# A decoder layer's opening: modulation sums on TensorE column tiles, and the first four FFN units taken row chunk by row chunk

## The reference

```python
cond = silu(c)
mod = cond @ w_ada + b_ada                    # 1024 x 9216: nine shifts, scales and gates
sh1, sc1, gt1, sh2, sc2, gt2, sh3, sc3, gt3 = split(mod, 9)
u = rms_norm(x, g_ffn1) * (1 + sc1) + sh1
a, b = split(u @ w_ffn1_in, 2)                # 1024 x 5632
h = x + 0.5 * gt1 * ((silu(a) * b) @ w_ffn1_out)
```

## Time and profile before

| | |
|---|---|
| three runs | 1361.37, 1361.68 and 1363.66 us, median 1361.68 us |
| the profiled execution | 1360.55 us |
| its span, first to last instruction | 1358.5 us |
| TensorE busy | 1261.8 us, 93% |
| VectorE busy | 668.1 us, 49% |
| ScalarE busy | 658.8 us, 48% |
| chain that ended last | TensorE 85%, VectorE 6%, ScalarE 5%, SyncE's queue 2%, DMA 1% |

### The profile page before, as it was taken

One profiled execution on the slowest core, in us unless ns is written; L12 is line 12 of the kernel. 1 busy time (PEld: TensorE's weight loads), 2 busy tenths in 40 slices (PEclk: granted clock), 3 DMA queues, 4 the chain that ended last, 5 costly groups with the idle time before them and its releaser, 6 DMA issues.

```text
span 1358.5 us, 17931 instructions
## 1 busy us (share of the span) xinstructions
PE 1261.8 (93%) x6505; PEld 1015.8 (75%) x6505; DVE 668.1 (49%) x953; ACT 658.8 (48%) x1152; POOL 69.7 (5%) x101
## 2 busy tenths in 40 slices
PE   2699999999997999999888978899799999999998
PEld 1588888887775777777667857677578888888887
DVE  6766666665443563665374345465453333333221
ACT  5566666665553696555684332653432232222221
POOL 3000000000110000000302121001100000000000
PEclk8699999999999999999998988999999999999999
DMA  9467776776552222222221120163223333343321
GB/s 322 114 186 186 184 187 184 187 199 178 147 156 62 62 78 78 63 62 78 78 70 47 48 70 25 61 182 117 83 62 99 102 93 93 98 124 97 114 79 31
DMA packets 279955, 152.36 MB, mean 112 GB/s; under 512 B 7877, under 2 KB 275294, under 8 KB 279902
## 3 DMA queue, kind: packets, MB, share of 16 engines
q1 hardware_dynamic: 275678, 149.54, 39.6%
q10 hardware_dynamic: 4224, 2.10, 0.5%
HBM read 145.31 MB, written 6.29 MB: 112 GB/s over the span
## 4 chain that ended last, share of the span: by engine, by line
PE 85%; DVE 6%; ACT 5%; SPq 2%; issue 2%; DMA 1%; ACTq 0%; DVEq 0%
PE region L1278 12%; PE region L1279 12%; PE region L1280 12%; PE tail L1278 12%; PE tail L1279 12%; PE tail L1280 12%; PE region L1434 2%; SPq L366 1%; PE region L1296 1%; PE region L1582 1%; PE region L1572 1%; PE region L1586 1%; PE region L1420 1%; PE region L1469 1%; PE region L1307 1%
## 5 line engine op out<-in xcount | busy, mean ns | idle before, releaser
L505 ACT ACTIVATE w_hi<-raw 128x1024 fp32r<-128x1024 f32 (+1 forms) x181 | 201.6, 1115 | 493.2 <-PE region L1280 242.4
L857 DVE TENSOR_TENSOR w_lo<-raw,w_hi 128x1024 fp32r<-128x1024 f32 (+1 forms) x181 | 234.9, 1298 | 270.7 <-ACT w_hi L505 269.1
L1278 PE MATMUL region<-u_hi,w_hi 128*128 128x512 f32 x672 | 265.7, 395 | 3.7 <-DVE w_lo L857 3.7
L1280 PE MATMUL region<-u_hi,w_lo 128*128 128x512 f32 x672 | 261.6, 389 | 0.0
L1279 PE MATMUL region<-u_lo,w_hi 128*128 128x512 f32 x672 | 261.6, 389 | 0.0
L1278 PE MATMUL tail<-u_hi,w_hi 128*128 128x512 f32 x344 | 145.7, 423 | 8.2 <-DVE w_lo L857 8.2
L1278 PEld LDWEIGHTS region<-u_hi,w_hi 128*128 128x128 f32 x672 | 126.1, 188 | 32.8 <-issue 4.7
L1279 PEld LDWEIGHTS region<-u_lo,w_hi 128*128 128x128 f32 x672 | 126.1, 188 | 28.3 <-issue 2.4
L1280 PEld LDWEIGHTS region<-u_hi,w_lo 128*128 128x128 f32 x672 | 126.1, 188 | 26.4
L1278 PE MATMUL tail<-g_hi,w_hi 128*128 128x512 f32 x352 | 141.1, 401 | 0.0
L1280 PE MATMUL tail<-g_hi,w_lo 128*128 128x512 f32 x352 | 139.0, 395 | 0.0
(11 more groups left out here) (285 smaller groups left out, 1531.4 us busy)
## 6 DMA issues: line engine op xcount, KB each, us to landing
raw<-in_w_ffn_in SPq DMA_DIRECT2D x176, 256.0 KB, 3.4
ada_raw<-in_w_ada SPq DMA_DIRECT2D x56, 512.0 KB, 5.1
raw<-in_w_in SPq DMA_DIRECT2D x90, 256.0 KB, 3.3
raw<-in_w_ffn_out SPq DMA_DIRECT2D x32, 384.0 KB, 4.6
raw<-in_w_ffn_out SPq DMA_DIRECT2D x32, 320.0 KB, 3.6
ada_early<-in_w_ada SPq DMA_DIRECT2D x8, 1024.0 KB, 12.0
kept_gates<-rstd SPq DMA_DIRECT2D x16, 256.0 KB, 3.6
gates<-kept_gates SPq DMA_DIRECT2D x16, 256.0 KB, 4.2
```

The source lines that it names most:

```text
L505: act.activation(w_hi[:, slot % 2, 0:k, :], raw[:, slot, 0:k, :], ACT.Copy).then_inc(hi_ready, 1)
L857: dve.tensor_tensor(w_lo[:, slot % 2, 0:k, :], raw[:, slot, 0:k, :], w_hi[:, slot % 2, 0:k, :].bitcast(f32), ALU.subtract).then_inc(lo_rea ...
L1278: pe.matmul(bank(b), wh, xh, start=start and n == 0, stop=False)
L1280: ins = pe.matmul(bank(b), wl, xh, start=False, stop=stop and n == k - 1)
```

## The change

Nothing outside the opening and the start of FFN1's first product is changed, apart from semaphore counts.

**Loads.** x comes first, with one semaphore for each block of 128 tokens. The small vectors follow. The eight early pieces come in the order scale, shift, scale, shift (256 columns each). Behind every second piece come two row chunks of the first four units, in four loads of 128 KB: 128 rows of four 128-column blocks.

**Root mean square.** ScalarE squares x as it lies in memory, with the sum along the row; Ln and Exp give the rough root for 512 tokens in a 128 x 4 tile, VectorE refines it, and four matmuls spread it. VectorE now copies the transposed x to `hT`.

**Early sums.** TensorE multiplies cond, broadcast to 32 columns, with a row chunk of a piece, in one of four column tiles of 32 columns; eight matmuls per piece, two in each tile. ScalarE copies the 128 x 256 result, and two matmuls with a column of 1/32 put the sums on partitions. `ada_sum` and the scaling and halving of early pieces are gone.

**Four units.** Units 0 to 3 are worked through with the row chunk outermost: `first_half(k, 0)` is chunk k of units 0 and 1, `first_half(k, 1)` of units 2 and 3, six matmuls each. The chunks of a pair have their weights and activations split in pairs on ScalarE and VectorE. The five places that the split weights of a chunk go through lie in the two `w` slots.

**Behind them.** The units of the pairs j = 0 and 1 are then finished together. With j = 0 ScalarE and VectorE split units 4 and 5; with j = 1 they split none; from j = 2 on they split two each as before (unit 6 first).

```diff
--- before.py
+++ after.py
+FIRST = 4
+F1_IN = KD - FIRST
...
+def first_tile(k):
+    return FIRST * ((k + 2) % 5)
+def early_col(a):
+    return PIECE * (a // 2) + (0 if a % 2 else D)
...
@@ sync @@
-            sp.dma_start(ada_early[:, 0], w_ada_v[:, :, 0:PIECE]).then_inc(ada_early_in[0], 16)
             for b in range(NB):
-                sp.dma_start(x_nat[:, b, :], x[0, b * P:(b + 1) * P, :]).then_inc(x_in, 16)
-            for q in range(1, EARLY):
-                sp.dma_start(ada_early[:, q], w_ada_v[:, :, q * PIECE:(q + 1) * PIECE]).then_inc(ada_early_in[q], 16)
+                sp.dma_start(x_nat[:, b, :], x[0, b * P:(b + 1) * P, :]).then_inc(x_in[b], 16)
...
-            for u in range(RAW):
-                load(F1_IN, 0, u)
+            for a in range(EARLY):
+                sp.dma_start(ada_early[:, a], w_ada_v[:, :, early_col(a):early_col(a) + PIECE]).then_inc(ada_early_in[a], 16)
+                if a % 2:
+                    for k in (a - 1, a):
+                        for half in range(2):
+                            sp.dma_start(raw_tiles[:, FIRST * k + 2 * half:FIRST * k + 2 * half + 2, :],
+                                         ffn_in_v[0][:, k, half * FF:half * FF + 2 * P].rearrange("p (t n) -> p t n", n=P))\
+                                .then_inc(first_in[k // 2], 16)
...
             for i in laps(sp, KF // 2):
+                if is_static(i) and i == 0:
+                    load(F1_IN, 0, 3 + RAW)
+                    for u, used in ((0, 2), (1, 5)):
+                        sp.wait_ge(lo_ready, used)
+                        load(F1_IN, 0, u + RAW)
+                        load_late(u, u)
+                    sp.wait_ge(lo_ready, KD)
+                    load(F1_IN, 0, 2 + RAW)
                 for u in range(4):
...
@@ scalar: ffn @@
-                        split_hi(phase, i, 2 * jj + 2)
-                        act.wait_ge(unit_done, phase + 2 * j + 1)
+                        lead = 2 * jj + 2 if f or not is_static(j) or j > 1 else 4 if j == 0 else None
+                        if lead is not None:
+                            split_hi(phase, i, lead)
+                        if lead == 2 * jj + 2:
+                            act.wait_ge(unit_done, phase + 2 * j + 1)
+                        elif j == 0:
+                            act.wait_ge(unit_done, KD)
+                        else:
+                            act.wait_ge(first_done, 1)
...
-                        split_hi(phase, i, 2 * jj + 3)
+                        if lead is not None:
+                            split_hi(phase, i, lead + 1)
@@ scalar: opening @@
+            act.preload_act_table_set("natural_log_exp_and_others")
+            for b in range(NB):
+                act.wait_ge(x_in[b], 16)
...
+                act.activation(x_sq[:, :], x_nat[:, b, :], ACT.Square, accum_out=tok["sum"][:, b:b + 1]).then_inc(tok_root, 1)
...
+            def early_part(a):
+                act.wait_ge(early_ps, a + 1)
+                if a >= 2:
+                    act.wait_ge(early_cols, a - 1)
+                act.activation(parts[:, a % 2, :], bank(6 + a % 2)[:, 0:PIECE], ACT.Copy).then_inc(early_copied, 1)
+            def first_hi(k):
+                act.wait_ge(first_in[k // 2], 64)
+                if k >= 5:
+                    act.wait_ge(unit_done, k - 4)
+                act.activation(wh_tiles[:, first_tile(k):first_tile(k) + FIRST, :],
+                               raw_tiles[:, FIRST * k:FIRST * k + FIRST, :], ACT.Copy).then_inc(hi_ready, 1)
+            early_part(0)
+            early_part(1)
+            for k in range(0, KD, 2):
+                first_hi(k)
+                first_hi(k + 1)
+                act.wait_ge(early_mod, k + 2)
+                for k1 in (k, k + 1):
+                    act.wait_ge(normed_ready, k1 + 1)
+                    act.activation(u_hi[:, k1, :], work[:, k1 % 2, :], ACT.Identity,
+                                   bias=mod[:, SH[0] * KD + k1:SH[0] * KD + k1 + 1]).then_inc(u_hi_ready, 1)
+                if k + 2 < KD:
+                    early_part(k + 2)
+                    early_part(k + 3)
@@ vector: opening @@
...
+            for k in range(0, KD, 2):
+                first_scale(k)
+                scaled(0, k)
+                early_columns(k + 1)
+                scaled(0, k + 1)
+                first_lo(k)
+                low(0, k)
+                first_lo(k + 1)
+                low(0, k + 1)
+                dve.wait_ge(u_lo_ready, k + 2)
@@ tensor: opening @@
...
+            def early_piece(a):
+                pe.wait_ge(ada_early_in[a], 16)
+                if a >= 2:
+                    pe.wait_ge(early_copied, a - 1)
+                for k in range(KD):
+                    t = k % 4
+                    ins = pe.matmul(bank(6 + a % 2)[32 * t:32 * t + 32, 0:PIECE],
+                                    cond[:, k:k + 1].to_broadcast([P, 32]), ada_early[:, a, k, :],
+                                    start=k < 4, stop=k >= 4, tile_position=(0, 32 * t))
+                ins.then_inc(early_ps, 1)
+            def early_totals(a):
+                pe.wait_ge(early_copied, a + 1)
...
+                for n in range(2):
+                    col = early_col(a) // P + n
+                    ins = pe.matmul(bank(5 - a % 2)[:, col:col + 1], parts[:, a % 2, n * P:(n + 1) * P], share[:, 0:1],
+                                    start=True, stop=True)
+                ins.then_inc(early_cols, 1)
+            def first_half(k, j):
+                if j == 0:
+                    pe.wait_ge(lo_ready, k + 1)
+                    pe.wait_ge(u_lo_ready, k + 1)
+                xh, xl = u_hi[:, k, :], u_lo[:, k, :]
+                for ab in range(2):
+                    tile = first_tile(k) + 2 * ab + j
+                    wh, wl, dst = wh_tiles[:, tile, :], wl_tiles[:, tile, :], bank(2 * j + ab)
+                    pe.matmul(dst, wh, xh, start=k == 0, stop=False)
+                    pe.matmul(dst, wh, xl, start=False, stop=False)
+                    ins = pe.matmul(dst, wl, xh, start=False, stop=k == KD - 1)
+                return ins
+            early_piece(0)
+            early_piece(1)
+            early_totals(0)
+            early_totals(1)
             for k in range(KD):
+                more = k % 2 == 0 and k + 2 < KD
+                ins = first_half(k, 0)
...
+                if more:
+                    early_piece(k + 2)
+                    early_piece(k + 3)
+                ins = first_half(k, 1)
+                ins.then_inc(first_done if k == KD - 1 else unit_done, 1)
+                if more:
+                    early_totals(k + 2)
+                    early_totals(k + 3)
             ffn_in(0, F1_IN)
```

More of the change, by code:

```diff
@@ L159, in build @@
         eps = sb("eps", [P, 1])
+        share = sb("share", [P, 1])
         ssq = sb("ssq", [P, S])
@@ L170, in build @@
             ada_early = sb("ada_early", [P, EARLY, KD, PIECE], stack=s)
+            parts = sb("parts", [P, 2, PIECE], stack=s)
+            x_sq = sb("x_sq", [P, D], stack=s)
+            tok = {n: sb("tok_" + n, [P, NB], stack=s) for n in ("sum", "mean", "rstd", "tmp")}
         with ExitStack() as s:
@@ L222, in bank @@
             return t[:, k * S:(k + 1) * S]
+        raw_tiles = raw.rearrange("p s k n -> p (s k) n")
+        wh_tiles, wl_tiles = (t.rearrange("p s k n -> p (s k) n") for t in (w_hi, w_lo))
         def heads(ap):
@@ L555, in ffn @@
                                 ada_scale(ada_raw[:, k], ada_scaled, (ada_in[k], 16 * (j + 1)))
-            act.wait_ge(masks, 9)
+            act.wait_ge(masks, 10)
             act.wait_ge(c_ps, 1)
[L560 to L565, removed]
@@ L576, in _ @@
             ffn(0, F1_IN)
-            for i in laps(act, KD // 2, 0, 1):
+            for i in laps(act, KD // 2):
                 for oo in range(2):
@@ L858, in split_lo @@
                                   w_hi[:, slot % 2, 0:k, :].bitcast(f32), ALU.subtract).then_inc(lo_ready, 1)
[L860 to L865, removed]
-                        dve.wait_ge(done, KD * q + k)
-                        ins = dve.scalar_tensor_tensor(acc, piece[:, k, :], cond[:, k:k + 1], acc, ALU.mult, ALU.add)
-                    ins.then_inc(done, 1)
             def halve(acc, piece, done, q):
@@ L1008, in _ @@
-            split_lo(F1_IN, 0, 0)
-            split_lo(F1_IN, 0, 1)
-            dve.wait_ge(early_ps, 1)
-            dve.wait_ge(vec_ready, 2)
-            dve.tensor_tensor(mod[:, 0:LATE], bank(5)[:, 0:LATE], vec[:, 0:LATE], ALU.add).then_inc(early_mod, 1)
-            dve.wait_ge(early_mod, 1)
-            norm(0)
+            for t in range(2 * NB):
+                b, half = t // 2, t % 2
+                dve.wait_ge(x_ps, t + 1)
+                dve.tensor_copy(hT[:, 4 * half:4 * half + 4, b * P:(b + 1) * P], heads(bank(t % 4))).then_inc(h_ready, 1)
@@ L1370, in _ @@
-            ins.then_inc(early_ps, 1)
```

(19 more changed lines are left out.)

201 lines of the change are left out of this document (111 added, 90 removed).

## The result

The changed kernel takes 1349.1 us (median; the runs lie between 1347.7 and 1351.4) against 1361.5 us before: ratio 0.9909, 95% interval 0.9889 to 0.9929. The forecast was 1348. The profiled execution took 1349.81 us, its span 1348.1.

A forecast was written before the change was run, and what follows sets the result against it. TensorE was taken to bound the kernel except in the opening, held by loads and VectorE. Ten units done at 98.3 instead of 111.7 us save 13.4: 1360.55 becomes 1347.1, as a median 1348; 80% range 1338 to 1363.

The forecast's parts named there:

- First FFN matmul: Opening, TensorE: the first FFN matmul starts at 22.5 us, 30 us earlier than before.
- Column tiles: Early sums on TensorE: four column tiles overlap fully, a piece taking 0.86 us at clock 1.00, 1.7 at half clock.
- the rival: Early sums: column tiles don't overlap fourfold; one after another a piece takes 3.4 us at 1.00, time 1366; chance 0.12.
- The loop: Opening, from pair to pair of chunks: TensorE's queue plus 3.9 us of VectorE's chain, 8.8 us a pair.
- The distance that the loads would have given: Opening: 7.6 us between pairs, a sign that the loads and not the loop bound it.
- Four units: End of the opening on TensorE: units 0 to 3 done at 57.2 us; 54 all at 1.00, up to 66.
- The new wait: Behind unit 5: unit 6 waits for late pieces, TensorE idle from T + 11.4 to T + 17.6 except a 0.86 us sum.
- T: The time at which the first four units are done on TensorE, forecast at 57.2 us.
- ten units: Units 0 to 9 done on TensorE: forecast T + 41.1 = 98.3 us, against 111.68 before.
- The half clock: Behind the pause after unit 5: TensorE's clock falls, and unit 6 and 7 lose 1.6 us.
- moves with it: Behind ten units: the same work, bound by TensorE, was to shift by the same 13.4 us.
- sum 2: The second late sum on TensorE, by which ten units are done; forecast 98.3 us, 111.68 before.

The follow-up runs named there:

- e3_lo_first: Changed kernel with VectorE making both `w_lo` of a pair of chunks ahead of the columns; 1348.87 us, ratio 0.9912 to before.
- e5_filled: Changed kernel with five unused f32 matmuls put into TensorE's pause ahead of the first late sum; 1345.56 us, ratio 0.9866 to before.
- a_again: The changed kernel run again without any edit; 1347.56 us, ratio 0.99 to before.
- e1_late_ahead: Changed kernel with scaling of late pieces 0 and 1 ahead of the first silu, their halving also earlier; 1341.97 us, ratio 0.9863 to before.
- e6_both: Changed kernel with the edits of e1_late_ahead and e3_lo_first together; 1344.86 us, ratio 0.9885 to before.
- e4_x_late: Changed kernel with SyncE asking for early pieces 0 and 1 ahead of x; 1351.3 us, ratio 0.9902 to before.
- e2_one_tile: Changed kernel without column tiles, a piece's eight matmuls one after another over 128 columns; 1367.08 us, ratio 1.0026 to before.

## Why the prediction was right, point by point

- **First FFN matmul.** Predicted 22.5 us, found 21.81, 21.55, 21.77 and 21.66 in four executions of this opening. The last link was as told: piece 1 seen late, its sums, then VectorE's columns, `work`, `w_lo` and `u_lo` (2.85 us for 2.9). The links ahead of it were off both ways: piece 1 was seen at 16.78 for 15.9, but its matmuls took 1.0 us for 1.7 and the sums 1.2 for 2.0, since TensorE's clock was 1.00 there (windows 16.7 to 19 us) and not 0.50.
- **Column tiles.** Predicted 0.86 us a piece for full overlap; found 1.93/2 = 0.97 at clock 1.00, against 7.07/2 = 3.5 without. The price of the rival was right too: 1366 predicted, 1367.08 found with the overlap gone. The Trainium skill, "TensorE: Matmul & The Clock Gate" (Part 3, Measured speedup vs the span model), has 2.38-fold for three column tiles; four gave 3.66-fold here, which lies between that share and full overlap. Of the 2 us that its share would have added, about 0.9 came (0.97 for 0.86 us, eight pieces).
- **The loop.** Predicted 8.8 us a pair, found 8.8. That the sum came out so well is luck. From the first sum to chunk 4's first matmul the forecast set 3.9 us for VectorE's chain; it took 3.3 (37.53 to 40.81), and the terms ahead of it were 0.6 us longer than forecast:

```profile
37.53 0.16 DVE L1087 TENSOR_TENSOR mod<-region,vec 128x2 f32<-128x2 f32 x1 [4.39 <-PE region L1495]
```

And the forecast had it that the chain counts and chunk k + 1 does not. In fact TensorE is at work on chunk k + 1 until 0.22 us before the chain ends, so the loop is TensorE's queue almost alone, with 0.15 us of VectorE's chain (e3_lo_first). The distance that the loads would have given, 7.6, does not appear.
- **Four units.** Predicted 57.2, found 55.2: 0.7 us from the first matmul, and 1.4 us of half clock in the first loop (10.2 against 8.8) in place of 2.9. The first six matmuls ran at 0.50 as forecast (windows 21.8 to 24.6 us), the pieces behind them mostly did not in this execution (0.94 from 24.6 to 27.8).
- **The new wait.** Predicted from T: piece 3 asked for at T + 8.1, unit 6 at T + 17.6, ten units at T + 41.1. With T = 55.2 that is 63.3, 72.8 and 96.3; found 63.29, 73.2 and 96.43. Of all steps this one was nearest: most of its links had a row of the same form in the trace before, and what had to be found was only who stands behind whom on ScalarE. One link was another: unit 6 was to wait for VectorE's split, which ended at 72.2, and it waited for the sum ahead of it, which at 0.50 took 2.08 us in place of 0.86 and ended at 73.2. The half clock cost 2.0 to 2.4 us (e5_filled) where 1.6 were set.
- **What the prediction left out.** It said that all behind ten units "moves with it". It does not quite. Between sum 2 and the end of the span, 1.5 to 5.3 us of the lead over the profiled execution of before are lost in all eight kernels:

| | lead at sum 2 | lead at the end | given back |
|---|---|---|---|
| the changed kernel | 15.25 | 10.4 | 4.8 |
| a_again | 14.0 | 11.9 | 2.1 |
| e1_late_ahead | 20.75 | 18.3 | 2.4 |
| e3_lo_first | 14.5 | 10.9 | 3.6 |
| e6_both | 20.8 | 16.3 | 4.5 |
| e4_x_late | 10.8 | 5.5 | 5.3 |
| e5_filled | 16.0 | 14.5 | 1.5 |
| e2_one_tile | -3.1 | -7.6 | 4.5 |

The lead can be followed by the same instructions in both traces. In the changed kernel it is 15.2 to 15.3 us until before's 450 us, and moves between 13.6 and 15.5, both ways, until 880. Two places then take the larger part of the 4.8 us. The first is a pause of the mixer, the one of the earlier trace rows: TensorE waits for VectorE's `ydn_lo`, this for ScalarE, and ScalarE for the transfer of `rstd` to `kept_gates`. ScalarE's and TensorE's timelines of before:

```profile
882.24 0.60 ACT L637 ACTIVATE rstd<-tail 128x512 f32<-128x512 f32 x1 [3.36 <-DMA kept_gates<-rstd]
884.13 0.50 PE L1278 MATMUL region<-ydn_hi,w_hi 128*128 128x512 f32 x1 [3.34 <-DVE ydn_lo L1237]
```

The same of the changed kernel:

```profile
868.50 0.60 ACT L712 ACTIVATE rstd<-tail 128x512 f32<-128x512 f32 x1 [5.14 <-DMA kept_gates<-rstd]
870.39 0.80 PE L1381 MATMUL region<-ydn_hi,w_hi 128*128 128x512 f32 x1 [5.12 <-DVE ydn_lo L1340]
```

From SyncE's issue to ScalarE's start it is 5.42 us (863.08 to 868.50) in place of 3.64 (878.60 to 882.24), the pause is 1.8 us longer, and the half clock behind it lasts 4.4 us in place of 3.3: the lead goes from 15.5 to 13.3 us. TensorE's pause is 5.1 to 5.6 us in seven of the eight kernels; in e5_filled, which gives back least, it is 3.39. Why the transfer is slow in seven kernels and fast in before and e5_filled is open, and before has one trace, so its other executions may differ.

The second place is the start of the second FFN. TensorE's timeline of before, the first matmul of its first two units and of the third:

```profile
984.49 0.77 PE L1307 MATMUL region<-u_hi,w_hi 128*128 128x512 f32 x1 [7.41 <-DVE u_lo L930]
...
998.90 0.47 PE L1278 MATMUL region<-u_hi,w_hi 128*128 128x512 f32 x1 [1.88 <-DVE w_lo L857]
```

The same of the changed kernel:

```profile
971.12 0.77 PE L1410 MATMUL region<-u_hi,w_hi 128*128 128x512 f32 x1 [7.41 <-DVE u_lo L1000]
...
987.02 0.47 PE L1381 MATMUL region<-u_hi,w_hi 128*128 128x512 f32 x1 [1.88 <-DVE w_lo L932]
```

The waits, 7.41 and 1.88 us, and the instructions are the same, but the stretch takes 14.41 us before and 15.90 after. The windows say why: the clock over the two units with the pause behind them, and over the next 4.1 us; first before, then after.

```profile
984.40:998.80 14.40, 12.53 (x48) 9.96 (x48) 10.45 (x14) 6.68 (x8) 0.00 (x0) 0.90 0.00 0
998.80:1002.90 4.10, 4.00 (x18) 3.33 (x19) 2.52 (x3) 2.06 (x3) 0.00 (x0) 1.00 0.44 129
```

```profile
971.00:986.90 15.90, 14.02 (x48) 11.02 (x48) 10.47 (x14) 6.67 (x8) 0.00 (x0) 0.80 0.00 0
986.90:991.00 4.10, 3.98 (x11) 3.14 (x12) 2.51 (x3) 2.08 (x4) 0.00 (x0) 0.58 0.44 129
```

After the 7.41 us pause the clock came back later, and it fell once more behind the next, shorter pause, which before it did not. Here the lead goes from 13.4 to 11.9 us and on to 10.2 (at 0.58 instead of 1.00, 4.1 us lose 1.7). That is a size of this execution rather than a cost of the change: in its repeat, the same program, the lead stays at 11.8 us over this place. e4_x_late loses 3.1 us here as well, the other kernels at most 0.3.

So the loss is not one thing: a longer wait for a transfer at the same place in seven of eight kernels, and half-clock stretches that fall otherwise from execution to execution. The table also compares each kernel with one execution of before, and the last three were run in the second set, where before's runs, but for the one of 3237.11, lie between 1359.82 and 1366.98 us. Against before's median there, e4_x_late ends 12.1 us ahead and e5_filled 17.8, more than at sum 2.

The time came out at 1349.1 for 1348 with two errors of opposite sign: ten units were done 1.9 us sooner than forecast, and 4.8 us were given back in the profiled execution, for which the sum had no term. That the forecast is off by only 1.1 us is therefore luck in part. The mechanism is not: the overlap (e2_one_tile), the new wait (e1_late_ahead) and the half clock behind it (e5_filled) were each shown by a run of their own.

## What to carry to other kernels

When work is moved earlier, follow each engine's written order past the place where the slack was: the late pieces, once hidden behind 22 us of TensorE's work, became a wait of 4.4 us because the first two were scaled behind a split on ScalarE, and moving their scaling ahead of the first silu was worth 5.6 us more. A wait in front of TensorE can have a second price in the clock behind it, here about 2 us for a pause of 4.5, so taking it away can give more than its length. And price a new use of an engine from the nearest rows in the trace, with what happens if it fails: without the overlap of the column tiles the whole gain was gone.

## What the runs showed of the hardware

- Eight f32 matmuls of 256 columns in four column tiles of 32 took 0.97 us at clock 1.00, and 3.5 us one after the other on the full width: 3.66-fold.
- The same opening got its full clock back at different points. With the first chunk at 21.81 and 21.77 us, the pair of pieces behind it took 2.07 us in the changed kernel (from 24.64; clock 0.94 from 24.6 to 27.8) and 3.15 in e1_late_ahead (from 24.60; clock 0.61); with the first chunk at 22.89 in both, 2.06 in e6_both and 3.06 in e3_lo_first. From the first chunk to unit 4 it is 33.7 us in the changed kernel (21.81 to 55.51), 34.7 in a_again (21.55 to 56.22) and 35.0 in e5_filled (21.66 to 56.61), with no edit in this stretch.
- The transfer of `rstd` to `kept_gates` ahead of the pause of the earlier trace rows took 3.64 us in before, 3.69 in e5_filled and 5.42 in the changed kernel, from SyncE's issue to ScalarE's start, with the same instructions around it.
